# Attention of two layers, reordered: diff maps and fox heads of each query tile taken in turn

## The reference, cut to what matters

```python
for l in range(2):                       # first block; 16 meta tokens + 512 tokens, width 1024
    proj = rmsnorm(h) @ w_in[l]          # dq, dk, dv, dg, fq, fk, fv, ff, fg
    # diff: 4 heads of 2 maps, head dim 64, values 128 wide; visible: chunk of key <= chunk of query
    p = softmax(q @ k.T / 8);  a = p[:, :, 0] - lam * p[:, :, 1]
    do = rmsnorm(a @ v) * subln_gain * (1 - lam_init) * silu(dg)
    # fox: 8 heads of 64; causal, with cumulative forget gates as a bias on the scores
    s = q @ k.T / 8 + c[query] - c[key];  fo = softmax(s) @ v * silu(fg)
    h = h + concat([do, fo]) @ w_out[l]
# second block: FFN, sparse and stick-breaking attention, memory attention, FFN
```

## Time and profile before

| | |
|---|---|
| median of three runs | 2051.18 us (2046.05 to 2056.36) |
| the profiled execution | 2039.61 us, its span 2037.8 us |
| busy PE, PEld | 1947.8 us (96%), 1667.1 us (82%) |
| busy DVE, ACT, POOL | 744.0 (37%), 723.7 (36%), 738.8 us (36%) |
| mean granted clock of PE | 0.964 |
| weights read | 140.40 MB, 70 GB/s over the span |

### The profile page before, as it was taken

The page is one execution under the profiler, slowest core; times in us unless marked ns, Lnnn a source line. Parts: engine busy times, 40 slices in busy tenths (PEclk is TensorE's granted clock), DMA queues, the critical chain, the costliest instruction groups (busy, mean ns, idle before and its releaser), DMA issues.

```text
span 2037.8 us, 27083 instructions
## 1 busy us (share of the span) xinstructions
PE 1947.8 (96%) x11102; PEld 1667.1 (82%) x11102; DVE 744.0 (37%) x1276; ACT 723.7 (36%) x1360; POOL 738.8 (36%) x370
## 2 busy tenths in 40 slices
PE   7999979999999799999999999999999989999999
PEld 7999868898997688788888877789867868888887
DVE  5322353353322644552111254546676441111001
ACT  3222343432223454323222222435565542222211
POOL 3543200145533012455554432330003425555543
PEclk9999776999999799999999999999999989999999
DMA  4222100022222001232233323210002202222233
GB/s 148 73 84 74 62 1 1 10 84 83 84 74 83 1 1 42 92 98 94 93 93 96 93 80 131 96 62 1 1 1 93 94 31 93 94 96 99 89 96 106
DMA packets 40586, 144.23 MB, mean 71 GB/s; under 512 B 4624, under 2 KB 4880, under 8 KB 40336
## 3 DMA queue, kind: packets, MB, share of 16 engines
q1 hardware_dynamic: 40464, 142.51, 21.8%
HBM read 140.40 MB, written 2.10 MB: 70 GB/s over the span
## 4 chain that ended last, share of the span: by engine, by line
PE 87%; DVE 7%; ACT 3%; issue 2%; DMA 1%; POOL 1%; SPq 0%; DVEq 0%; ACTq 0%
PE ps L365 22%; PE ps L366 22%; PE ps L367 22%; PE ps L881 6%; PE ps L842 5%; PE ps L869 3%; PE ps L2037 1%; DMA raw<-wstream 1%; DVE nm L921 1%; PE ps L2020 1%; PE ps L1000 1%; PE ps L492 1%; DVE xl L421 1%; PE ps L1781 1%; DVE scratch L470 1%
## 5 line engine op out<-in xcount | busy, mean ns | idle before, releaser
L361 POOL TENSOR_TENSOR wl<-raw,wh 128x1024 fp32r<-128x1024 f32 (+2 forms) x254 | 604.2, 2379 | 829.4 <-ACT wh L353 829.4
L365 PE MATMUL ps<-xh,wh 128*128 128x512 f32 (+1 forms) x1728 | 621.6, 360 | 25.7 <-POOL wl L361 12.2
L366 PE MATMUL ps<-xl,wh 128*128 128x512 f32 (+1 forms) x1728 | 615.3, 356 | 0.0
L367 PE MATMUL ps<-xh,wl 128*128 128x512 f32 (+1 forms) x1728 | 613.0, 355 | 0.0
L353 ACT ACTIVATE wh<-raw 128x1024 fp32r<-128x1024 f32 (+2 forms) x254 | 266.1, 1048 | 961.8 <-PE ps L367 893.4
L365 PEld LDWEIGHTS ps<-xh,wh 128*128 128x128 f32 x1728 | 326.6, 189 | 81.0 <-issue 18.3
L366 PEld LDWEIGHTS ps<-xl,wh 128*128 128x128 f32 x1728 | 326.8, 189 | 49.9 <-issue 2.2
L367 PEld LDWEIGHTS ps<-xh,wl 128*128 128x128 f32 x1728 | 327.2, 189 | 48.1
L1127 POOL TENSOR_TENSOR xl<-xb,xh 128x512 fp32r<-128x512 f32 (+1 forms) x22 | 26.1, 1186 | 377.2 <-ACT xh L1036 377.2
L921 DVE TENSOR_REDUCE nm<-ps 128x1 f32<-128x144 f32 (+7 forms) x208 | 99.2, 490 | 111.7 <-PE ps L842 111.6
L367 PE MATMUL ps<-aH,wl 128*128 128x512 f32 x352 | 138.2, 393 | 0.0
(11 more groups left out here) (350 smaller groups left out, 2630.2 us busy)
## 6 DMA issues: line engine op xcount, KB each, us to landing
raw<-wstream SPq DMA_DIRECT2D x236, 512.0 KB, 3.5
raw<-wstream SPq DMA_DIRECT2D x16, 384.0 KB, 3.0
raw<-wstream SPq DMA_DIRECT2D x10, 528.0 KB, 3.5
h<-xT SPq DMA_DIRECT2D x4, 528.0 KB, 5.8
out<-h SPq DMA_DIRECT2D x8, 256.0 KB, 4.0
hm<-memT SPq DMA_DIRECT2D x1, 1024.0 KB, 4.7
cst<-const SPq DMA_DIRECT2D x1, 720.5 KB, 9.0
cst<-const SPq DMA_DIRECT2D x1, 320.0 KB, 4.0
```

Of the source, the lines that this page charges most:

```text
L361: e.tensor_tensor(wl[p % 2][:, 0:n], raw[c % 2][:, 0:n], wh[p % 2][:, 0:n].bitcast(F32), ALU.subtract).then_inc(*w_lo(p))
L365: e.matmul(o, w_h, x_h, start=start, stop=False)
L366: e.matmul(o, w_h, x_l, start=False, stop=False)
L367: return e.matmul(o, w_l, x_h, start=False, stop=stop)
```

## The change

1. `layer_plan` runs over tiles 3, 2, 1, 0, and in a tile over diff 0, fox 1, diff 1, fox 0, diff 2, fox 3 and so on: a diff map and a fox head on the other half of the rows are a pair of `begin`. Fox's forget term goes first in its list. `begin` pairs two lists of unequal length, so that the longer one's last matmuls run alone; the mask products come last.
2. Jobs: fox 2 steps after its unit, a diff pair 4 steps after its second map (unit u − 2 and u). The mix comes one step later, after the next maximum. Flips, jobs and buffers are numbered by the step of the transposition.
3. Diff's product stays in bank 6, fox's in bank 7, for all tiles; what an end transposes goes to banks 4 and 5 (`turn_at`), which the flips use too. Diff's end first copies the raw product out (ACT), squares the copy into `fin`, and scales the copy.
4. The probabilities of both kinds lie in the place of the layer's features and outputs: slots in the first four of its 16 rows of 528 columns, the two `PT` in columns 0 to 127 of the next ten. An output's halves wait for the last diff product of their tile. The row sums get four places instead of two.
5. Layer 0's meta tokens start at steps 36 (diff) and 47 (fox); their outputs wait in `rst` until step 68.
6. The output projection takes slices 4 to 7 first, then 0 to 3, and waits for tile 0.

```diff
-        P_of = {(0, "diff"): (Pb0, PT0), (0, "fox"): (Pb1, PT1), (1, "diff"): (Pb1, PT1), (1, "fox"): (Pb0, PT0)}
+        over = [over0, over1]
+        P_of = {l: ([over[l], scratch], [over[l][:, 4 + 5 * i:9 + 5 * i, 0:128] for i in range(2)]) for l in range(2)}
...
-                for u, x in enumerate(units):
-                    if x.job:
+                for u in sorted((u for u in range(n) if units[u].job), key=lambda u: u + units[u].job):
+                    x = units[u]
...
-                    for ta, tb in zip(units[a].terms, units[b].terms):
-                        ra = part(pa, units[a], ta)
-                        rb = part(pb, units[b], tb)
-                    ra.then_inc(*score(name, a))
-                    rb.then_inc(*score(name, b))
+                    for ta, tb in zip_longest(units[a].terms[:-1], units[b].terms[:-1]):
+                        if ta:
+                            part(pa, units[a], ta)
+                        if tb:
+                            part(pb, units[b], tb)
+                    part(pa, units[a], units[a].terms[-1]).then_inc(*score(name, a))
+                    part(pb, units[b], units[b].terms[-1]).then_inc(*score(name, b))
...
-                if s < len(units) and units[s].pair:
+                u = s - 1
+                if 0 <= u < len(units) and units[u].pair:
...
-                e.activation(osb[0:nq, f, 0:512], PS[0:nq, 512 * b:512 * b + 512], ACT.Square).then_inc(
-                    *a_end(*key, "sq"))
+                d = osb[0:nq, f, 0:512]
+                e.activation(d, PS[0:nq, 512 * b:512 * b + 512], ACT.Copy).then_inc(*a_end(*key, "raw"))
+                fin_free(on, before)
+                on.wait_ge(*a_end[key + ("raw",)])
+                e.activation(fin[0:nq, f, 0:512], d, ACT.Square).then_inc(*a_end(*key, "sq"))
...
+        def halves_act(e, on, plan, key, u):
...
+            on.wait_ge(*v_end[key + ("gate",)])
+            if u is not None:
+                on.wait_ge(*pv[plan.name, u])
...
-            for kind in ("diff", "fox"):
-                (Qh, Ql), (Kh, Kl) = QK[kind[0] + "q", l], QK[kind[0] + "k", l]
-                V, hd = (VA, 128) if kind == "diff" else (VB, 64)
-                for i in range(4):
...
+            ends = [("diff", 3), ("fox", 3), ("diff", 2), ("fox", 2)]
+            ends += [("diff", -1), ("fox", 1), ("diff", 1), ("fox", -1)] if l == 0 else [("diff", 1), ("fox", 1)]
+            for kind, i in ends + [("diff", 0), ("fox", 0)]:
+                order[kind, l, i] = len(order)
+            for i in (3, 2, 1, 0):
+                n, c0, wide, beside_meta = M + 128 * (i + 1), M + 128 * i, i == 3, l == 0 and i < 2
+                for kind in ("diff", "fox"):
+                    out_at[kind, l, i], turn_at[kind, l, i] = (6, 4) if kind == "diff" else (7, 5)
+
+                for m, kind in [(m + (kind == "fox") * (1 - 2 * (m % 2)), kind) for m in range(8) for kind in ("diff", "fox")]:
...
+                        cols=(hd * hh, hd * hh + hd), ahead=(1 if wide else 2) + second, rows=True, places=P_of[l],
+                        job=2 if second else 4 if m % 2 else 0, pair=not second and m % 2 == 1,
+                        third=1000 if second else 4, first=m == 1, last=m == (6 if second else 7), out_bank=out_at[key]))
...
+                begins = [(36, ("meta", "diff", l), 5 + END_STEPS["diff"]), (47, ("meta", "fox", l), 5 + END_STEPS["fox"]),
+                          (68, ("put", "diff", l), 1), (68, ("put", "fox", l), 1)]
...
-            return lambda k: [s["ao", "diff" if k < 4 else "fox", l, 3] for s in (x_hi, x_lo)]
+            return lambda k: [s["ao", "diff" if k < 4 else "fox", l, 0] for s in (x_hi, x_lo)]
...
-            for _ in residual_pe(e, on, ("wout", l), layer_ao(l), n, c0, pair, X[l]):
+            for _ in residual_pe(e, on, ("wout", l), layer_ao(l), n, c0, pair, X[l], (4, 5, 6, 7, 0, 1, 2, 3)):
```

More of the change, by code:

```diff
@@ L2 @@
 from contextlib import ExitStack
+from itertools import zip_longest
 import numpy as np
@@ L182, in program @@
         d_x = [sem(f"d_x{i}") for i in range(4)]
-        def flipped(name, at):
-            sb("before" + name, [128, 4, L], at=at)
-            P = sb("Pb" + name, [128, 4, L], at=at)
-            sb("between" + name, [128, 4, L], at=at)
-            return P, [sb(f"PT{name}{i}", [128, 640], at=at) for i in range(2)]
         h = sb("h", [128, KT, L])
@@ L378, in feature_tile @@
             for i in range(halves):
-                for k in range(nk):
+                for k in ks:
                     for s in x(k):
@@ L812, in source @@
             def source(self, u):
-                return self.slot(u - 1 if self.units[u].pair else u)
+                return self.slot(u - 2 if self.units[u].pair else u)
             def slot_read(self, u):
@@ L822, in slot_read @@
                     return mixed[self.name, was]
-                return flip[self.name, was if self.units[was].job else was + 1]
+                return flip[self.name, was if self.units[was].job else was + 2]
             def bank(self, u):
@@ L876, in attention_pe @@
                     if x.first:
-                        claim(on, x.out_bank, 1, v_end[x.group + ("scaled",)])
+                        claim(on, x.out_bank, 1, a_end[x.group + ("raw",)] if x.group[0] == "diff" else v_end[x.group + ("scaled",)])
                     on.wait_ge(*plan.copied(u))
@@ L969, in turned, with ending, fin_free, outputs_put @@
         def turned(key, ntile, nq):
-            b = out_at[key]
+            b = turn_at.get(key, out_at[key])
             return PS[:, 512 * b:512 * b + 128 * ntile].rearrange("p (a b) -> p a b", a=ntile)[:, :, 0:nq]
-        def ending(f, ntile, nq):
-            return fin[:, f, 0:ntile * nq].rearrange("p (a b) -> p a b", a=ntile)
+        def ending(key, ntile, nq):
+            if nq == 16:
+                a = 256 if key[0] == "diff" else 320
+                return rst[:, a:a + 64].rearrange("p (a b) -> p a b", a=ntile)
+            return fin[:, place(key)[0], 0:ntile * nq].rearrange("p (a b) -> p a b", a=ntile)
+        def fin_free(on, before):
+            if before and before[0] in ("diff", "fox") and before[2] < 0:
+                if before[0] == "diff":
+                    on.wait_ge(*v_end[before + ("ms",)])
+                else:
+                    fin_free(on, place(before)[1])
+            elif before:
+                on.wait_ge(*x_hi[("ao",) + before])
+                on.wait_ge(*x_lo[("ao",) + before])
+        def outputs_put(key):
+            return {"diff": 5, "fox": 2, "mem": 2, "nsa1": 5}.get(key[0])
         def ends_in(key):
@@ L1095, in end_dve @@
                         return
-                    u = (key[2] + 1 if kind == "fox" else key[1]) % 2
+                    u = key[2] % 2 if kind == "fox" else key[1] % 2
                     on.wait_ge(*pv[plan.name, last_unit[key]])
@@ L1099, in end_dve @@
                         on.wait_ge(*turn[before])
-                    e.reciprocal(rr[:, u, 0:heads], rs[:, u, 0:heads]).then_inc(*v_end(*key, "recip"))
+                    e.reciprocal(rr[:, u, 0:heads], rs[:, u + 2 * (kind == "fox"), 0:heads]).then_inc(*v_end(*key, "recip"))
                     on.wait_ge(*v_end.now())
@@ L1208, in program @@
         META_BANK = 3
-        JOB = {"diff": 3, "fox": 2}
         last_unit = {}
         def layer_plan(l):
-            units, begins, groups = [], [], []
+            units, begins = [], []
             used = {b: -1 for b in range(4)}
```

198 lines of the change are left out of this document (94 added, 104 removed).

## The result

The changed kernel took 2,061.08 us in the median of 10 runs (2,056.78 to 2,063.98), the kernel before in the same comparison 2,048.50 us (10 runs, 2,043.25 to 2,056.36). The ratio is 1.0061, 95% interval 1.0046 to 1.0076: slower by some 13 us, where 27 us less were forecast. That is inside the range of 1,992 to 2,070 us, on the side that had a chance of 0.19. The profiled execution of the changed kernel took 2,060.6 us with a span of 2,058.8 us. Between the two profiled spans lie 21 us, because the execution of before that was profiled was 9 us under its own median.

What follows compares the result with a forecast made beforehand. PE bounds the fox phases; in diff phases PE, DVE and ACT wait for one another, with 128 of 299 us at half clock. Gain 62 us less 35 taken back by the clock, 27 us: 2,051.2 to 2,024 us, range 1,992 to 2,070.

Steps and rivals of the forecast that it cites:

- The sum at full clock: Attention at full clock: layer 1 at 112 us against 134.4, layer 0 at 126 us against 165.8.
- Together 62 us: Gain of both layers' attention at full clock: 22 us in layer 1 plus 40 us in layer 0.
- what the clock takes back: Loss to half clock: 7 + 7 us in tile 3, 15 at meta products, 6 in restarts before the projection; 35 us.
- I take 15 us: Half-clock loss from layer 0's 64 meta products of 16 columns in tile 1: 15 us.
- Tiles 2, 1, 0: Small tiles at full clock, bound by PE: 60.7 us plus six turned outputs and waits, 66 us per layer.
- My 40.4 us for tile 3: Wide tile at full clock: start of 8.6 us plus 6 loops of 5.3 us, per layer.
- Three banks: Layer 0: having three score banks costs an estimated 2 us.
- The open ends: Last diff end before the projection: uncovered wait of 5.5 us in layer 1 and 6.8 us in layer 0.
- Lone slots: Score slots running alone on half the rows, 40 per layer: taken as free; the skill's rule gave 16 us for both layers.
- The clock stays low: Rival, chance 0.19: clock falls in tile 3 and stays down through tiles 3 and 2; 2,063 to 2,116 us.
- my three signs of being wrong: Wide loops over 12 us at full clock; small tiles under 85% PE at clock 1.0; tiles 3 and 2 clock under 0.6.
- Waits in order: Rival, chance 0.20: ten extra PE waits of about 2 us per layer give back 20 us; 2,044 us, no measurable change.

Runs made afterwards that it cites:

- e3: The changed kernel without layer 0's meta-token attention, three score banks kept: 2,027.9 us, ratio 0.9901 to the kernel before.
- e15: e3 with all four score banks in tiles 1 and 0 of layer 0: 2,014.3 us, ratio 0.9837 to the kernel before.
- e16: The changed kernel with three score banks only for layer 0's units 38 to 57, four for the other units: 2,055.1 us, ratio 1.0048.
- e7: The changed kernel with the output projection reading its slices in the order 0 to 7 (diff first): 2,065.8 us, ratio 1.0098.
- e14: The changed kernel with meta-token attention done in layer 1 too, with three score banks there: 2,110.0 us, ratio 1.0316.
- e2: The changed kernel with 18 extra full-height products of 384 columns, before and beside the meta scores: 2,071.6 us, ratio 1.0114.
- e11 to e13: Two 400-column products ahead of each pair's scores in layer 0's small tiles, in changed kernel, e1 (tile 2 too), kernel before: 2,070.8, 2,063.4, 2,053.9 us.
- e1: The changed kernel with layer 0's meta tokens begun at steps 20 and 31, beside tile 2: 2,056.0 us, ratio 1.0044.
- e4: The kernel before without layer 0's meta-token attention: 2,020.2 us, ratio 0.9863.
- e9: The kernel before with each kind's tiles in the order 3, 2, 1, 0 and meta tokens beside tile 1: 2,070.1 us, ratio 1.0101.
- e10: The changed, mixed kernel with tiles in the order 0, 1, 2, 3 and meta tokens beside tiles 0 and 1: 2,070.4 us, ratio 1.0128.
- e6: The changed kernel with mixing undone (eight diff units, then eight fox units per tile; projection slices 0 to 7): 2,093.8 us, ratio 1.0208.

## Why the prediction was wrong, step by step

**The sum at full clock: 4% low, and misread.** It gave 112 + 126 = 238 us. Idle and work of the two layers measured 118.0 + 129.9 = 247.9. The same two parts of the kernel before are 114.5 + 127.7 = 242.2, so where the sum promised 4 us less, the kernel got 5.7 us more. Of the 62 us that I booked as gain, 56.5 were before's own clock (36.6 + 19.9), which leaves 5.5 for all that the change does (1.4 of it the wait ahead of layer 0's projection). The step "Together 62 us" compared a sum at full clock with measured lengths, and so put nearly the whole forecast on the smaller number behind it, what the clock takes back.

**That number failed.** Inside the attentions I took 7 + 7 for tile 3 and 15 for the meta products, 29 us. Measured: 53.6 + 11.3 = 64.9. Tile 3 was near (36.64 × 0.28 = 10.3 and 36.83 × 0.26 = 9.6). The term that failed is "I take 15 us": tiles 1 and 0 of layer 0 lost 40.16 × 0.32 + 51.57 × 0.47 = 37 us. I had sized it by the stretch of 29.5 us in the earlier trace rows. In the new order the stretch was not 29.5 but 89 us long, with one exception of 3.5 us. The prediction left the meta attention's price as it was while everything around it moved, and that was the mistake. Tile 2 of layer 0 lost another 33.01 × 0.13 = 4.3 us. I also read the earlier trace rows wrongly in one point: the fall behind the 1.6 us at 272 and the 29.5 us from 312.5 on are two different stretches, with the clock back at full from 292 to 302 and from 305.5 on. And the 2,051.2 us that I subtracted from, the median of three runs, was 2.7 us above that of the ten.

**Tiles 2, 1, 0: 66 us forecast, 77.5 at clock 1.00 in layer 1.** The scores fit (1.20, 0.97 and 0.88 us a pair, from start to start, against 1.2, 1.0 and 0.88). The groups of PE from 715.71 to 793.20 show what else is there:

```profile
L881 PE MATMUL ps<-VB,over 128*128 128x64 f32 x174 | 23.9, 275 | 0.5 <-ACT over L908 0.5
L881 PE MATMUL ps<-VA,over 128*128 128x128 f32 x92 | 12.8, 277 | 0.9 <-ACT over L908 0.9
...
L869 PE MATMUL ps<-identR,scratch 128*128 128x128 f32 x69 | 10.2, 275 | 0.8 <-ACT over L908 0.8
...
L869 PE MATMUL ps<-identR,over 128*128 128x128 f32 x54 | 7.9, 274 | 0.0
```

Twelve jobs of 4, 3 and 2 blocks are 108 transposes and 216 value products; the rows have 123 and 266. The surplus is the tail of the wide tile, whose last jobs come after its scores. By the earlier trace rows a transpose takes 0.57 / 5 = 0.11 us and a value product 1.06 / 10 = 0.11, so it is 15 + 50 of them, 1.7 + 5.3 = 7.0 us. My 40.4 us for tile 3 held its start and its loops, and no line held its tail. The other 4.5 us of the difference I have not traced; PE was idle for 3.1 us in these tiles, and I had allowed some 2.6 for waits.

**Three banks: 2 us forecast, 15 measured** between e3 and e15, half of it clock. With the meta tokens there, e16 got 11.5 us of layer 0 back (6.0 by the medians) with 12 of 32 units on four banks.

**Right:** a pair of wide loops at full clock takes 5.65 us (261.85 to 267.50) and then 5.08 (to 272.58), together 10.7, forecast 10.6. Tile 3 took 44.5 and 45.5 us, forecast 40.4 + 7. PE was busy 97, 98 and 92% of tiles 2 to 0 in layer 1; the mean clock of the whole layer is 0.90. Work rose by 4.3 us in layer 1, forecast 4 for the wider score slots; in layer 0, by the table, it did not rise (109.7 to 108.9), by the finer cut by 1.0. The open ends are 4.20 + 0.52 us and 4.20 + 0.69, forecast 5.5 and 6.8; e7 bears out that the fox slices cover the rest. Their place was wrong: there is no wait for POOL of 3 to 4 us in the first projection tile, since PE's list has the last turned diff output ahead of the projection, and PE waits for that (the row at 798.68).

**Lone slots.** A mixed pair's scores take 1.60 us in the wide tile (261.85 to the first transpose at 263.45), as a fox pair's did (1.59). In tile 0 it is 0.88 us for both. The lone slots cost nothing that can be seen in these. The Trainium skill ("TensorE: Matmul & The Clock Gate", Part 3, The mechanism) lets a weight load overlap only matmuls of other row groups; the 16 us that this rule gave for both layers did not come, so the measurement decides against using it here.

**The rivals.** "The clock stays low" was the right kind: from the mean clocks 121 + 26 = 147 us stood at half, and the kernel came out slower, where I had put the turning point at 150. But I placed it in tiles 3 and 2, where the clock averaged 0.72 to 1.00; it came in tiles 1 and 0, and only in the layer with meta tokens. So none of my three signs of being wrong showed (wide loops over 12 us at full clock, small tiles under 85% busy at full clock, tiles 3 and 2 under a clock of 0.6), though layer 0 took 183.5 us and not 146. "Waits in order" was not it: PE's idle time in both layers went from 35.3 to 37.5 us.

**What stays open.** e3 and e14 show that the meta attention, with its bank, brings the clock down, and e3 and e15 that the missing bank does some of it alone. Why it then stays down so long is not settled; longer products did not prevent it (e2, e11 to e13). The traces give a lead. In all ten executions in which the clock was full when fox's 40 meta scores of 16 columns began, it fell some 2 to 4 us later, whatever tile they lay beside (before: 308.7 and 312.5). In eleven of the sixteen kernels with meta tokens it came back 7 to 13 us behind their last product (before: 335.5 and 343.0; e1: 356.0 and 364; e14: 823.3 and 830.5). The changed kernel is one of the eleven:

```profile
386.19 0.60 PE L1020 MATMUL ps<-identR,tmpn 16*128 16x16 f32 x4
```

```profile
326.00:394.00 68.00, 63.54 (x314) 55.58 (x313) 22.44 (x76) 19.11 (x66) 2.54 (x2) 0.50 0.00 1
394.00:397.50 3.50, 2.79 (x26) 2.42 (x25) 1.40 (x7) 2.27 (x9) 1.26 (x1) 0.99 0.00 0
```

So its first 68 us at half clock cover the meta attention from near its start (324.0) to just behind its end. Small tiles as such do not hold the clock down: in e1 tile 0 of layer 0 ran at 1.00. And the mixing has brought diff's and fox's meta tokens together, 324.0 to 354.1 and 360.3 to 386.2, in a part of the layer that would run at full clock, whereas in the kernel before diff's (232.6 to 251.9) lie in the slow start, where e4 is at half clock without any. That would double their price as the split of e3 and e4 shows it. It is a reading of the traces that no run here tests, and the order of the tiles is its rival: reversing it cost the unmixed kernel 25.5 us of clock (e9), but undoing it gained the mixed one nothing (e10). And one execution's clock is partly chance: nine kernels whose layer 1 is the changed one's show it at 129.2 to 134.6 us, five with before's at 132.1 to 136.9. The 5 us that layer 1 won are thus more like 2.5 (means 132.1 and 134.6).

## What to carry to other kernels

When you price a reordering by a sum at full clock, split the kernel before in the same way (idle, work, clock) ahead of taking the difference; a gain that is all clock must be argued stretch by stretch, from what will surround each stretch in the new order. A small piece of work that a change only moves along can still change its price: look at the clock around it before, and ask what will surround it now. And count a pipeline's tail once for every place where the size of its stages shrinks.

## What the runs showed that I had not expected

- TensorE at half clock while it is busy nearly without a hole: in e9 51.92 of 53.00 us at 0.50, the row above. The Trainium skill ("TensorE: Matmul & The Clock Gate", Part 1, What's actually happening) says that the clock follows how busy PE has been recently. The trace does not agree if busy means the share of time with a matmul under way: layer 1 of the changed kernel kept 1.00 through tile 0 with PE busy 92%.
- A product of 16 columns behind a new weight load every 0.11 us at full clock comes every 0.21 us at half. Such products are not spared by having few columns.
- Some programs differ far more from run to run than others, and the mean clock goes with the time: e6 took 2,073.8 to 2,106.2 us in six runs, at mean clocks from 0.951 down to 0.933, the changed kernel 2,056.8 to 2,064.0 in ten.
